# A delta-rule recurrence: the last level of the triangular inverse multiplies its 64x64 blocks alone

## The chip, the core and the metric

The kernel runs on one core of one Trainium2 chip. The metric is the device time in microseconds (us) of one launch, the median over runs. TensorE (PE in the profile; PEld is its weight load) multiplies from SBUF into PSUM; VectorE (DVE) and ScalarE (ACT) read PSUM and compute; GpSimd (POOL) computes on SBUF; SyncE (SP) starts transfers.

## What is computed

The launch computes a whole transformer block with three mixers (attention, a state-space mixer, a gated delta-rule mixer) and then a second block. The change lies in the delta-rule mixer. Cut to what matters:

```
def gdn_mixer(qkv, z, b, a, conv_w, dt_bias, a_log, norm_w):
    ...
    kbeta = kc * betac[..., None]
    strict = jnp.tril(jnp.einsum('bhcid,bhcjd->bhcij', kbeta, kc) * decay, -1)
    rhs = jnp.concatenate([vc * betac[..., None], kbeta * jnp.exp(gc)[..., None]], axis=-1)
    sol = lax.linalg.triangular_solve(strict, rhs, left_side=True, lower=True, unit_diagonal=True)
    u, w = jnp.split(sol, [GDN_HEAD_V], axis=-1)
    ...
    def step(state, inp):
        v_new = u_i - jnp.einsum('bhld,bhde->bhle', w_i, state)
        o = ...
        state = ...
```

There are 1024 tokens and 4 heads. The kernel works with 8 chunks of 128 tokens, so each chunk and head has one 128x128 unit lower triangular matrix whose inverse is wanted.

## The kernel before

All engines walk one list of items, written in `schedule`, each engine issuing in that order its own part of each item. An item of the delta pass is named by a kind and a chunk c:

- `gx` (ACT, L1910): expands the four inverted 32x32 diagonal blocks of chunk c into the 128x128 tiles X (the inverse so far) and XT (its transpose), zero elsewhere.
- `ly` (c, level): TensorE multiplies the triangular matrix (in `SQ[c]`) by X for 4 heads into one PSUM bank (L1467); DVE writes it, times a 0/1 mask of the blocks of that level, to Y (L2499). Level 5 joins 32x32 blocks into 64x64 ones, level 6 joins the two 64x64 blocks into the whole.
- `lx` (c, level): TensorE multiplies Y and X in both orders (L1479), and DVE subtracts the results from X (L2506) and XT (L2508). At level 6 only XT is wanted, so only that product is made.
- `uw` (c): TensorE multiplies the finished XT by the right-hand sides (L1503, then L1506, whose weights have 64 columns and whose result lies on 64 partitions, the halves taken in turn); ACT copies the result (L1921).
- `r1` and `r2` (c): the recurrence. TensorE multiplies by the state (L1513, L1515), DVE makes v_new (`vn`, L2513) and L2514; TensorE multiplies by vn (L1519, L1521); DVE adds up the output (L2518), masks the state's update (L2519) and adds it to the state `Sbd` (L2521). ACT then takes the output's squares (L1897).

The text calls the level 6 items ly6 and lx6, the level 5 items ly5 and lx5. All products are float32, and the trace shows two MATMUL records (passes), each with its weight load, for each such matmul call; an item of 4 heads has 8 passes. The order around the change is fixed by these lines, one round for each chunk c:

```
    for c in range(NT):
        s += at("gx", c + 3) + at("ly", c + 1, 6) + at("r1", c) + at("ly", c + 2, 5) + at("lx", c + 1, 6) + at("r2", c)
        s += at("lx", c + 2, 5) + at("uw", c + 1)
        s += [("gn", n) for n in range(len(NORMED) - 1) if NORMED[n] == c] + [("sn", 1)] * (c == 1)
```

Round c thus begins with ly6 of chunk c+1. `sn` and `gn` are 12 small DVE instructions each, a reciprocal square root of the norms, between two rounds; after `sn`, ACT scales a part of the state-space result (L1893). Ahead of the rounds stands a prologue with ly5, lx5, ly6, lx6 of chunk 0 and uw of chunk 0. Products go round robin through 4 PSUM banks. Before an item an engine waits for the counter of the product or copy that it needs.

Of the kernel before, what the change touches and what calls it, by code (L numbers as in the profile page):

```python
# [19 lines left out]
ALU = mybir.AluOpType  # L20
# [3 lines left out]
P = 128  # L24
# [42 lines left out]
C_ID, C_UP, C_BLK, C_B32, C_LV, C_NEG, C_ALI = 0, 128, 256, 384, 512, 768, 896  # L67
# [254 lines left out]
def build_program(nc, a, out):  # L322
# [166 lines left out]
    with ctx:  # L489
# [14 lines left out]
        con = sbuf("con", [C_END], 96)  # L504
# [58 lines left out]
        SQ = [sbuf(f"SQ{c}", [4, 2, P], 4 * c) for c in range(NT)]  # L563
# [21 lines left out]
        X = [sbuf(f"X{i}", [4, P], 172 + 6 * i) for i in range(3)]  # L585
        XT = [sbuf(f"XT{i}", [4, P], 174 + 6 * i) for i in range(3)]
        Y = [sbuf(f"Y{i}", [4, P], 176 + 6 * i) for i in range(3)]
# [335 lines left out]
        def hslice(c):  # L923
            return slice(c * P, (c + 1) * P)
# [9 lines left out]
        def four(b):  # L934

            return b[:].rearrange("p (h n) -> p h n", h=4)
# [6 lines left out]
        def over(ap, m):  # L943

            return ap.unsqueeze(1).to_broadcast([P, m, ap.shape[1]])
# [250 lines left out]
        def _(pe):  # L1196
            mm, tr = nc.tensor.matmul, nc.tensor.transpose
# [123 lines left out]
            for it in sched:  # L1321
# [11 lines left out]
                elif kind == "cols":  # L1333
                    pe.wait_ge(con_loaded, 16 * 11)
                    b = bank((it, 0))
                    done(tr(b[:, 0:109], rows[0:109, :], ident[0:109, 0:109]), (it, 0))
                elif kind == "norm":
                    stage, hf = j
                    pe.wait_ge(N["diag_ready"], 2 * stage + hf + 1)
                    for k in range(KD):  # L1340
                        b = bank((it, k))
                        for i in range(4):
                            c = 4 * hf + i
                            last = mm(b[:, hslice(i)], norm_row(stage, c)[:, hslice(k)], diag[:, c, :], start=True, stop=True)
                        done(last, (it, k))
                elif kind == "nk":
# [3 lines left out]
                    b = gemm_bank(it)  # L1350
                    for c in range(4):
                        last = mm(b[:, hslice(c)], norm_row(2, c)[:, hslice(j)], diag[:, c, :], start=True, stop=True)
                    last.then_inc(gemm_done[gemm_use[it][1]], 1)
                elif kind == "mx":
# [3 lines left out]
                    for k in range(KD):  # L1358
                        b = bank((it, k))
                        for i in range(4):  # L1360
                            c = 4 * j + i
                            src = atts[:, c, hslice(k)] if k < 2 else xs[:, c, hslice(k - 2)] if k < 6 else qkv[:, c, hslice(k - 6)]
                            last = tr(b[:, hslice(i)], src, ident)
                        done(last, (it, k))
                elif kind == "smT":
                    gemm_consumed(pe, unit_of["sm", 0])
                    b = bank((it, 0))
                    src = stage_of(("sm", 0))[1]
                    for c in range(NT):
                        last = tr(b[:, 16 * c:16 * c + 16], src[0:16, hslice(c)], ident[0:16, 0:16])  # L1370
                    done(last, (it, 0))
                elif kind == "acs":
                    pe.wait_ge(N["da_ready"], 1)
                    pe.wait_ge(rest_loaded, 16)
                    b = bank((it, 0))
# [11 lines left out]
                elif kind == "as":  # L1387
# [3 lines left out]
                    for p in range(2):  # L1391
                        b = bank((it, p))
                        for kv in range(2):
                            last = mm(b[:, kv * 256:kv * 256 + 256], aqT[:, p, hslice(j)], akT[:, kv, j * P:j * P + 2 * P],
                                      start=True, stop=True)
                        done(last, (it, p))
                elif kind == "ap":
                    pe.wait_ge(N["att_exp"], j + 1)
                    for p in range(2):
                        b = bank((it, p))  # L1400
                        for i in range(4):
                            last = tr(b[:, hslice(i)], asb[:, 2 * p + i // 2, hslice(i % 2)], ident)
                        done(last, (it, p))
                elif kind == "ao":
# [5 lines left out]
                    b = bank((it, 0))  # L1410
                    for i in range(4):
                        p, kv = i // 2, i % 2
                        h = p + 2 * kv
                        for s in range(2):
                            last = mm(b[:, h * 64:h * 64 + 64], apT[:, i, s, :], av[:, j + s, kv * 64:kv * 64 + 64],
                                      start=s == 0, stop=s == 1)
                    done(last, (it, 0))
                elif kind in ("pa", "sa"):
                    c = j
                    for key in products_of(it):  # L1420
                        b = bank((it, key))
# [5 lines left out]
                        for h in range(4):  # L1427
                            last = mm(b[:, hslice(h)], da[:, c, 4 * i + h:4 * i + h + 1].to_broadcast([P, P]), upper,
                                      start=False, stop=h == 3)
                        done(last, (it, key))  # L1430
                elif kind == "sg":
                    b = bank((it, 0))
                    for g in range(2):
                        last = mm(b[:, hslice(g)], BC[:, g, hslice(j)], BC[:, 2 + g, hslice(j)], start=True, stop=True)
                    done(last, (it, 0))
                elif kind in ("rk", "rj"):
                    c, z = j, j % 2
                    for key in products_of(it):
                        b = bank((it, key))
                        if key == "kT":  # L1440
# [3 lines left out]
                            for p in range(2):  # L1444
                                last = tr(b[:, hslice(2 + p)], kb[z][:, hslice(p)], ident)
                        elif key == "qT":
                            for p in range(2):
                                last = tr(b[:, hslice(p)], qkv[:, c, hslice(p)], ident)
                        elif key[:2] == "kq":
# [4 lines left out]
                            for h in range(2):  # L1454
                                mm(b[:, h * 256:h * 256 + P], kTp[z][:, 2 * p + h, :], kk[z][:, p, :], start=True, stop=True)
                                last = mm(b[:, h * 256 + P:h * 256 + 256], kTp[z][:, 2 * p + h, :], qT[:, c, p, :], start=True, stop=True)
                        done(last, (it, key))
                elif kind == "ly":
                    c, lv = j
                    z = c % 2  # L1460
# [3 lines left out]
                        side_consumed(pe, (("lx", (c, 5)), "x"))  # L1464
                    b = bank((it, 0))
                    for h in range(4):
                        last = mm(b[:, hslice(h)], SQ[c][:, h, 0, :], X[c % 3][:, h, :], start=True, stop=True)  # L1467
                    done(last, (it, 0))
                elif kind == "lx":
                    c, lv = j  # L1470
# [4 lines left out]
                    for key in products_of(it):  # L1475
                        b = bank((it, key))
                        for h in range(4):
                            l, r = (XT, Y) if key == "x" else (Y, XT)
                            last = mm(b[:, hslice(h)], l[c % 3][:, h, :], r[c % 3][:, h, :], start=True, stop=True)  # L1479
                        done(last, (it, key))  # L1480
                elif kind in ("uw", "yo", "yd", "st", "r1", "r2"):
                    c, z = j, j % 2
# [550 lines left out]
        def _(dve):  # L2033
            step = Steps(dve, dve_step)
            v = nc.vector
# [203 lines left out]
            for it in sched:  # L2239
# [256 lines left out]
                elif kind == "ly":  # L2496
                    c, lv = j
                    b = side_product(dve, (it, 0))
                    step.frees(v.tensor_tensor(Y[c % 3][:], four(b), over(con[:, C_LV + (lv - 5) * P:C_LV + (lv - 4) * P], 4), ALU.mult), (it, 0))  # L2499
                elif kind == "lx":  # L2500
                    c, lv = j
                    z = c % 3
# [2 lines left out]
                        b = side_product(dve, (it, "x"))  # L2505
                        step.frees(v.tensor_tensor(X[z][:], X[z][:], four(b), ALU.subtract), (it, "x"))  # L2506
                    b = side_product(dve, (it, "t"))
                    step.frees(v.tensor_tensor(XT[z][:], XT[z][:], four(b), ALU.subtract), (it, "t"))  # L2508
                elif kind == "r1":
                    c, z = j, j % 2  # L2510
                    side_consumed(dve, (("uw", c), 0))
# [131 lines left out]
```

## Time and profile before

| | |
|---|---|
| time, 3 runs | median 2302.89 us (2302.21 to 2303.53) |
| span of the profiled execution | 2301.8 us |
| TensorE busy | 2126.3 us (92%) |
| VectorE busy | 1236.5 us (54%) |
| the delta pass | from about 516 to 600 us of the span |

The page gives the profiled execution's span and no separate time for it; the span is 1.1 us below the median of the runs. Times in the trace count from the start of the span. The rounds of the delta pass start at 529.5 (c = 0), 540.4, 548.7, 558.1, 569.2, 578.7 and 587.05 us (c = 6); round 7 has only r1 and r2. Behind it stand the transposes for the output projection and the projection itself.

### The profile page before, as it was taken

The numbers are of one execution on the slowest core, as the hardware profiler recorded it, in microseconds if no ns is written. First come the engines' busy times: TensorE is split into PE (matmuls) and PEld (weight loads), VectorE is DVE, ScalarE is ACT, GpSimd is POOL, SyncE is SP. The second block draws the span as 40 slices with busy tenths as digits, with TensorE's granted clock in tenths as the row PEclk, the third lists the DMA queues.
The fourth block names the chain that finished last, engine by engine and source line by source line (L and its number), as shares of the span: only waits on it lengthen the run. The fifth ranks groups of instructions, "written<-read, shape, count | busy, mean of one in ns | idle before, by whom it ended". The sixth has DMA issues, their size and how long they took to land. (4 is left out here: it accounts for less than half of the span.)

```text
span 2301.8 us, 29448 instructions
## 1 busy us (share of the span) xinstructions
PE 2126.3 (92%) x10799; PEld 1783.6 (77%) x10799; DVE 1236.5 (54%) x1827; ACT 864.8 (38%) x1562; POOL 890.8 (39%) x612
## 2 busy tenths in 40 slices
PE   6999998868998999999999968889999999999997
PEld 6788877758886788888877757768888888888886
DVE  4443503866537843444489897679995245110232
ACT  4332216456324434343444544238774122000112
POOL 1232331331345688888832643220000333333334
PEclk9999998889999999999999988999999999999999
DMA  4111310011132122222274534200001111111131
GB/s 147 46 46 46 83 55 19 19 46 38 43 104 85 35 55 65 74 64 74 82 248 142 188 100 147 93 28 1 1 1 33 46 46 37 55 46 47 55 119 73
DMA packets 181824, 157.43 MB, mean 68 GB/s; under 512 B 27589, under 2 KB 147121, under 8 KB 181553
## 3 DMA queue, kind: packets, MB, share of 16 engines
q1 hardware_dynamic: 163904, 119.05, 17.4%
q10 hardware_dynamic: 17776, 36.51, 4.3%
q8 instruction: 86, 1.41, 0.3%
q14 instruction: 58, 0.47, 0.1%
HBM read 134.03 MB, written 21.50 MB: 68 GB/s over the span
## 5 line engine op out<-in xcount | busy, mean ns | idle before, releaser
L1118 POOL TENSOR_SCALAR w_hi<-w_raw 128x1024 fp32r<-128x1024 f32 x91 | 106.0, 1165 | 942.3 <-issue 893.6
L1230 PE MATMUL gemm<-h_hi,w_hi 128*128 128x512 f32 x1072 | 422.4, 394 | 5.6 <-POOL h_lo L1147 5.6
L1232 PE MATMUL gemm<-h_hi,w_lo 128*128 128x512 f32 x1072 | 418.2, 390 | 0.0
L1231 PE MATMUL gemm<-h_lo,w_hi 128*128 128x512 f32 x1072 | 418.0, 390 | 0.0
L1230 PEld LDWEIGHTS gemm<-h_hi,w_hi 128*128 128x128 f32 x1072 | 202.0, 188 | 49.6 <-issue 9.1
L1232 PEld LDWEIGHTS gemm<-h_hi,w_lo 128*128 128x128 f32 x1072 | 201.6, 188 | 42.5
L1231 PEld LDWEIGHTS gemm<-h_lo,w_hi 128*128 128x128 f32 x1072 | 202.1, 189 | 40.4
L1121 POOL TENSOR_TENSOR w_lo<-w_raw,w_hi 128x1024 fp32r<-128x1024 f32 x91 | 230.0, 2527 | 7.6
L870 POOL TENSOR_TENSOR w_lo<-wsum,w_hi 128x512 fp32r<-128x512 f32 x122 | 165.6, 1358 | 83.1 <-ACT w_hi L1682 77.8
L1682 ACT ACTIVATE w_hi<-wsum 128x512 fp32r<-128x512 f32 x155 | 98.1, 633 | 142.0 <-PE gemm L1310 60.8
L1308 PE MATMUL gemm<-h_hi,w_hi 128*128 128x512 f32 x320 | 124.5, 389 | 0.0
L1309 PE MATMUL gemm<-h_lo,w_hi 128*128 128x512 f32 x320 | 124.5, 389 | 0.0
L1310 PE MATMUL gemm<-h_hi,w_lo 128*128 128x512 f32 x320 | 124.5, 389 | 0.0
L2093 DVE SCALAR_TENSOR_TENSOR cacc<-cin,cols,cacc 128x1024 f32<-128x1024 f32 x42 | 67.0, 1596 | 90.1 <-ACT cacc L1630 89.1
L861 POOL TENSOR_TENSOR wsum<-w_raw 128x512 f32<-128x512 f32 x55 | 81.1, 1475 | 79.6 <-DVE w_lo L870 76.3
L870 POOL TENSOR_TENSOR w_lo<-w_raw,w_hi 128x512 fp32r<-128x512 f32 x62 | 88.4, 1425 | 43.8 <-ACT w_hi L1682 26.2
L1308 PE MATMUL gemm<-cmb,w_hi 128*128 128x512 f32 x240 | 94.2, 393 | 2.9 <-POOL w_lo L870 2.9
L1668 ACT ACTIVATE sig<-gemm,cols 128x1024 f32<-128x1024 f32 x16 | 18.0, 1124 | 210.0 <-PE gemm L1232 210.0
L1309 PE MATMUL gemm<-cmb,w_hi 128*128 128x512 f32 x240 | 93.9, 391 | 0.0
L1310 PE MATMUL gemm<-cmb,w_lo 128*128 128x512 f32 x240 | 93.8, 391 | 0.0
L2062 DVE TENSOR_TENSOR PT<-side,PT 128x512 fp32r<-128x512 f32 x128 | 88.5, 691 | 9.9 <-ACT PT L2004 5.9
L2004 ACT ACTIVATE PT<-side 128x512 fp32r<-128x512 f32 x128 | 76.6, 599 | 44.2 <-PE side L1552 39.6
(435 smaller groups left out, 4662.9 us busy)
## 6 DMA issues: line engine op xcount, KB each, us to landing
w_raw<-in_ffn_w_down SPq DMA_DIRECT2D x132, 256.0 KB, 3.1
w_raw<-in_w_in SPq DMA_DIRECT2D x60, 512.0 KB, 3.8
w_raw<-in_ffn_w_gate SPq DMA_DIRECT2D x22, 512.0 KB, 4.0
w_raw<-in_ffn_w_up SPq DMA_DIRECT2D x22, 512.0 KB, 4.1
w_raw<-in_w_out SPq DMA_DIRECT2D x16, 512.0 KB, 3.8
xin<-in_x SPq DMA_DIRECT2D x8, 512.0 KB, 6.9
x<-in_x ACTq DMA_DIRECT2D x1, 4096.0 KB, 15.7
x_spill<-x ACTq DMA_DIRECT2D x2, 2048.0 KB, 6.6
```

The lines of the kernel that those rows point to most:

```text
L861: step(ops.tensor_tensor(wsum[sum_of[n]["buf"]][:], x, y, op), "w_sum" if who == "pool" else "w_sum_v")
L870: ops.tensor_tensor(quarter(wlo, slot), x, quarter(whi, slot), ALU.subtract).then_inc(w_split, 1)
L1118: gp.tensor_scalar(hi[:], raw[key % 4][:], 1.0, 0.0, ALU.mult, ALU.add).then_inc(pool_hi, 1)
L1121: gp.tensor_tensor(lo[:], raw[key % 4][:], hi[:], ALU.subtract).then_inc(w_split, 1)
L1230: mm(o, hi[:, k, m], act[0][:, k, t], start=k == 0, stop=False)
L1231: mm(o, hi[:, k, m], act[1][:, k, t], start=False, stop=False)
L1232: last = mm(o, lo[:, k, m], act[0][:, k, t], start=False, stop=k == kt - 1)
L1308: mm(o, hi[:, k, :], b[0], start=k == 0, stop=False)
L1309: mm(o, hi[:, k, :], b[1], start=False, stop=False)
L1310: last = mm(o, lo[:, k, :], b[0], start=False, stop=k == 3)
L1682: step(af(quarter(whi, slot), x, ACT.Copy), "w_quarter_hi")
L2062: ins = v.tensor_tensor(dst, b, hi, ALU.subtract)
```

## The change

At level 6 only one 64x64 block of each product is not masked off or known: rows 64 to 127, columns 0 to 63 of Y, and in XT rows 0 to 63, columns 64 to 127. The changed kernel multiplies only the 64x64 blocks: ly6 takes its operands from partitions 0 to 63 and writes PSUM partitions 64 to 127; lx6 takes them from 64 to 127 and writes 0 to 63. DVE copies 64 columns for each head on 64 partitions in place of the masked multiplication over 128 (no mask is needed), and writes the negated product to XT's empty block in place of a subtraction over all of XT. Level 5 is as before.

```diff
@@ ly, TensorE
                     for h in range(4):
-                        last = mm(b[:, hslice(h)], SQ[c][:, h, 0, :], X[c % 3][:, h, :], start=True, stop=True)
+                        if lv == 5:
+                            last = mm(b[:, hslice(h)], SQ[c][:, h, 0, :], X[c % 3][:, h, :], start=True, stop=True)
+                        else:
+                            last = mm(b[64:P, h * P:h * P + 64], SQ[c][0:64, h, 0, 64:P], X[c % 3][0:64, h, 0:64], start=True, stop=True)
@@ lx, TensorE
-                            last = mm(b[:, hslice(h)], l[c % 3][:, h, :], r[c % 3][:, h, :], start=True, stop=True)
+                            if lv == 5:
+                                last = mm(b[:, hslice(h)], l[c % 3][:, h, :], r[c % 3][:, h, :], start=True, stop=True)
+                            else:
+                                last = mm(b[0:64, h * P + 64:(h + 1) * P], Y[c % 3][64:P, h, 0:64], XT[c % 3][64:P, h, 64:P], start=True, stop=True)
@@ ly, VectorE
-                    step.frees(v.tensor_tensor(Y[c % 3][:], four(b), over(con[:, C_LV + (lv - 5) * P:C_LV + (lv - 4) * P], 4), ALU.mult), (it, 0))
+                    if lv == 5:
+                        step.frees(v.tensor_tensor(Y[c % 3][:], four(b), over(con[:, C_LV:C_LV + P], 4), ALU.mult), (it, 0))
+                    else:
+                        step.frees(v.tensor_copy(Y[c % 3][64:P, :, 0:64], four(b)[64:P, :, 0:64]), (it, 0))
@@ lx, VectorE
-                    step.frees(v.tensor_tensor(XT[z][:], XT[z][:], four(b), ALU.subtract), (it, "t"))
+                    if lv == 5:
+                        step.frees(v.tensor_tensor(XT[z][:], XT[z][:], four(b), ALU.subtract), (it, "t"))
+                    else:
+                        step.frees(v.tensor_scalar(XT[z][0:64, :, 64:P], four(b)[0:64, :, 64:P], -1.0, None, ALU.mult), (it, "t"))
```

TensorE's order from uw of chunk 0 to r2 of chunk 0, in the kernel before (the last numbers are rows by columns of what is written and the number of matmul calls; tile numbers tell the three buffers of X, XT, Y apart):

```order
L1503 MATMUL side<-kbv_163,XT_155 128x64 x4
L1506 MATMUL side<-XT_155,kbv_163 64x128 x4
L1467 MATMUL side<-X_153,SQ_119 128x128 x4
L1513 MATMUL side<-Sbd,uw_161 128x128 x2
L1515 MATMUL side<-Sbd,qT 128x128 x2
L1467 MATMUL side<-X_154,SQ_120 128x128 x4
L1479 MATMUL side<-XT_156,Y_159 128x128 x4
L1519 MATMUL side<-vn,SQ_118 128x64 x4
```

The same place in the changed kernel, whose line numbers behind the edit are higher:

```order
L1509 MATMUL side<-kbv_163,XT_155 128x64 x4
L1512 MATMUL side<-XT_155,kbv_163 64x128 x4
L1470 MATMUL side<-X_153,SQ_119 64x64 x4
L1519 MATMUL side<-Sbd,uw_161 128x128 x2
L1521 MATMUL side<-Sbd,qT 128x128 x2
L1468 MATMUL side<-X_154,SQ_120 128x128 x4
L1485 MATMUL side<-XT_156,Y_159 64x64 x4
L1525 MATMUL side<-vn,SQ_118 128x64 x4
```

Nothing moved: the third and seventh rows (ly6 and lx6) became 64x64 products, and each now stands between products of other shapes.

VectorE's order from ly6's copy to the state's update, before:

```order
L2499 TENSOR_TENSOR Y_159<-side,con 128x512
L2513 TENSOR_TENSOR vn<-uw_161,side 128x256
L2514 TENSOR_TENSOR o_168<-side,eacs 128x256
L2499 TENSOR_TENSOR Y_160<-side,con 128x512
L2508 TENSOR_TENSOR XT_156<-XT_156,side 128x512
L2518 TENSOR_TENSOR qkv<-o_168,side 128x256
L2519 TENSOR_TENSOR tS<-side,con 128x256
```

and the same in the changed kernel:

```order
L2508 COPY Y_159<-side 64x4x64
L2525 TENSOR_TENSOR vn<-uw_161,side 128x256
L2526 TENSOR_TENSOR o_168<-side,eacs 128x256
L2506 TENSOR_TENSOR Y_160<-side,con 128x512
L2520 TENSOR_SCALAR XT_156<-side 64x4x64
L2530 TENSOR_TENSOR qkv<-o_168,side 128x256
L2531 TENSOR_TENSOR tS<-side,con 128x256
```

Again the order is the same, and the first and the fifth row have 256 elements on each of 64 partitions where they had 512 on each of 128.

## Rows read from the trace of the kernel before

**Rows 1.** The page: the span and the engines' busy time.

```profile
span 2301.8 us, 29448 instructions
...
PE 2126.3 (92%) x10799; PEld 1783.6 (77%) x10799; DVE 1236.5 (54%) x1827; ACT 864.8 (38%) x1562; POOL 890.8 (39%) x612
```

**Rows 2.** Busy time in stretches, by round; PEclk is the granted clock.

```profile
core 0: us, PE busy (x) PEld busy (x) DVE busy (x) ACT busy (x) POOL busy (x), PEclk, DMA share, GB/s
...
540.40:548.70 8.30, 8.30 (x79) 8.06 (x77) 6.34 (x12) 5.21 (x17) 1.84 (x3) 1.00 0.00 0
548.70:558.10 9.40, 8.55 (x78) 8.14 (x76) 8.34 (x24) 6.52 (x14) 1.84 (x3) 1.00 0.01 2
558.10:569.20 11.10, 8.57 (x78) 8.16 (x76) 6.38 (x12) 7.96 (x29) 1.84 (x3) 1.00 0.00 1
...
587.00:594.70 7.70, 6.28 (x58) 5.80 (x55) 5.20 (x14) 2.59 (x10) 0.00 (x0) 1.00 0.00 0
594.70:601.50 6.80, 6.10 (x29) 5.83 (x28) 3.57 (x14) 0.97 (x6) 4.03 (x6) 0.50 0.01 2
```

**Rows 3.** Timeline of TensorE's weight loads, 538 to 549 us.

```profile
538.73 0.97 PEld L1503 LDWEIGHTS side<-kbv,XT 128*128 128x128 f32 x8
539.77 0.42 PEld L1506 LDWEIGHTS side<-XT,kbv 128*64 128x64 f32 x8
540.36 0.97 PEld L1467 LDWEIGHTS side<-X,SQ 128*128 128x128 f32 x8 [0.17 <-DVE X L2506]
541.24 0.53 PEld L1513 LDWEIGHTS side<-Sbd,uw 128*128 128x128 f32 x4
...
542.14 0.97 PEld L1467 LDWEIGHTS side<-X,SQ 128*128 128x128 f32 x8
543.03 0.97 PEld L1479 LDWEIGHTS side<-XT,Y 128*128 128x128 f32 x8
543.92 0.97 PEld L1519 LDWEIGHTS side<-vn,SQ 128*128 128x128 f32 x8
...
548.68 0.97 PEld L1467 LDWEIGHTS side<-X,SQ 128*128 128x128 f32 x8 [0.17 <-DVE X L2506]
```

**Rows 4.** What TensorE waited for, 516 to 602 us.

```profile
PE side L1467 <- ACT XT L1910: 4.6, 2, 2.4
PE side L1513 <- issue: 2.5, 1, 2.5
PE side L1479 <- DVE Y L2499: 1.8, 2, 0.9
```

**Rows 5.** Timeline of VectorE, end of round 1 and into round 2.

```profile
545.64 0.42 DVE L2518 TENSOR_TENSOR qkv<-o,side 128x256 f32<-128x256 f32 x1 [0.62 <-PE side L1521]
...
546.56 1.27 DVE L2521 SCALAR_TENSOR_TENSOR Sbd<-Sbd,cdc,tS 128x128 f32<-128x128 f32 x2
547.86 0.69 DVE L2506 TENSOR_TENSOR X<-X,side 128x512 f32<-128x512 f32 x1
...
549.30 0.17 DVE L2048 TENSOR_SCALAR nv<-nss_s 128x8 f32<-128x8 f32 x1
...
551.53 0.17 DVE L2054 SCALAR_TENSOR_TENSOR nrs_s<-nt__74,nrs_s 128x8 f32<-128x8 f32 x1
551.73 0.69 DVE L2499 TENSOR_TENSOR Y<-side,con 128x512 f32<-128x512 f32 x1
```

**Rows 6.** Timeline of ScalarE in rounds 2 and 3.

```profile
551.79 4.30 ACT L1893 ACTIVATE xs<-xs,nrs_s 128x256 f32<-128x256 f32 x8 [2.33 <-DVE nrs_s L2054]
...
561.11 0.60 ACT L1921 ACTIVATE uw<-side 128x512 f32<-128x512 f32 x1
```

**Rows 7.** VectorE's groups by shape, whole span: mean ns of one.

```profile
L2062 DVE TENSOR_TENSOR qp<-side,qp 64x512 fp32r<-64x512 f32 x16 | 11.1, 695 | 7.4 <-ACT qp L1979 7.1
...
L2457 DVE COPY qT<-side 128x256 f32<-128x256 f32 x8 | 3.4, 425 | 17.7 <-PE side L1448 17.7
```

**Rows 8.** The one line whose products use few rows of the array.

```profile
L1370 PE MATMUL side<-con,cacc x8: 207/208/230, 229.2 to 229.7; 16*128 16x16 f32 x8
```

## Prediction

> **What bounds the kernel.** I read the page first: TensorE is busy for 92% of a span of 2301.8 us [rows 1], so the first question for a change to TensorE's work is whether its own stretch is also TensorE's. The table by rounds says so, with exceptions. Round 1 (540.4 to 548.7) has TensorE busy 8.30 of 8.30 us at the full clock, 2.4 GHz (PEclk 1.00); rounds 2 and 3 take 9.40 and 11.10 us for the same 8.6 us of products [rows 2]. Then the waits: in the whole delta pass TensorE waits 4.6 us for ACT's expansion of X and XT, 2.5 us (once) at L1513, and 1.8 us (twice) for Y [rows 4]. The 2.5 us stand under "issue", but the timeline names the cause: L1513 reads uw, and ACT's copy of it ran at 561.11 to 561.71, behind ACT's 4.30 us of L1893 [rows 6]. So a shorter product pays where TensorE is back to back, and is lost just before one of these waits. The reader should also see a second loop almost as long as TensorE's: behind r2, DVE runs L2518 (545.64), L2519, two of L2521 and L2506 until 548.55, and ly6 of the next round needs that last one; its weights load at 548.68 [rows 5, 3]. This loop starts at r2's end, so what r2 gains it gains too: it caps nothing that comes ahead of r2.
>
> **What the change takes away on TensorE.** An item of 8 passes with full tiles takes 0.88 to 0.89 us from its first weight load to the next item's (540.36 to 541.24, 542.14 to 543.03, 543.03 to 543.92) [rows 3]. 16 such items (ly6 and lx6 of 8 chunks) become 64x64. No row of before shows a 64x64 product. The nearest is L1506: 64 columns of weights, all 128 rows, 8 loads within 0.42 us [rows 3]; I take 0.055 a pass, 0.44 an item. The other neighbour, L1370, has 16 rows and 128 columns of weights: 8 passes start within 0.5 us, some 0.065 each [rows 8], so 0.5 an item. The upper bound is that nothing shrinks (0.89): L1506's passes go to two halves of the array in turn, the new ones all to the same quarter, and if a load could then not run beside the product before it, the time would stay. The lower bound is half my value, 0.22, if the two passes of a call could run side by side. I take 0.44, since L1506's moving operand has 128 columns and the new one 64, which leaves room even where each tile works alone. The saving is 0.45 an item.
>
> **What it adds on TensorE.** Going from full tiles into narrow ones and back is not free. From L1503's first load (538.73) to L1513's (541.24) are 2.51 us; 2 x 0.89 of it is full items and 0.43 is L1506's, so 0.30 is left for two changes of shape, 0.15 each [rows 3]. ly6 stands behind L1506, so before it there was a change already; it adds one, on leaving. lx6 stands between full items and adds two, unless TensorE waits ahead of it anyway and the entry hides in the wait. So in a round that TensorE bounds ly6 gives 0.45 - 0.15 = 0.30 and lx6 0.45 - 0.30 = 0.15.
>
> That is a rule of the skill too, and it speaks against the change. The Trainium skill, "TensorEngine Tiling (Array Packing)", section Key Properties, says that a change of the tiling mode, as against a change of tile within one mode, drains TensorE; it gives no price. The trace agrees, with 0.15 us for each change. Without the drains the change would be worth 0.45 at every item, with them two thirds of that at ly6 and one third at lx6. The Trainium skill, "TensorE: Matmul & The Clock Gate", section LDWEIGHTS, has a load's time go with its columns (P/1.2 ns) and not with its rows: 64 columns would be 53 ns, an estimate of 0.43 us for 8, beside L1506's 0.42.
>
> **VectorE.** The two instructions of level 6 go from 512 elements a partition to 256. A copy of 128x256 out of PSUM takes 425 ns, and one of 64x512 takes 695 ns, as long as the 690 of the full ones [rows 7, 5], so the gain is in the columns and not in the partitions: 0.27 each, 4.3 us over 16. DVE is busy 6.34 of 8.30 us in round 1 [rows 2]; XT's write has lx5 and most of uw's time ahead of its reader, so it gives nothing on the path. Y's copy is on the path only where DVE is late: in rounds 2 and 4, where `sn` and `gn` keep DVE from 549.30 to 551.70 (and 2.5 us at 569.8) and lx6 waits 0.9 us for Y [rows 5, 4]. Scheduling, waits, banks and transfers are as before.
>
> **The sum by rounds** (what comes through to the end of the pass):
> - Prologue: ly6, ly5, lx6, lx5 of chunks 0 and 1. TensorE alone would gain 0.45; lx5's wait for DVE's copy of ly5's product leaves about 0.27. uw of chunk 0 and with it ACT's expansion behind it come 0.27 earlier.
> - Round 0: ly6 stands ahead of a wait for ACT of 2.2 us (half of the 4.6) and is lost, lx6 gives 0.15.
> - Round 1: 0.30 + 0.15 = 0.45. Here DVE's `sn` hangs on it, and so ACT's long chain.
> - Round 2: Y's copy 0.27 and lx6 0.30 (its entry hides in the wait), but all of it, and ly6 of round 3, is lost in the wait for ACT at 561.8, which runs from 551.79 without a gap [rows 6]. 0.
> - Round 3: lx6 0.15.
> - Round 4: 0.27 + 0.30 = 0.57. Round 5: 0.45.
> - Round 6: no ly5 between r1 and lx6, so Y's copy is just late as well (587.05 on): about 0.6.
> Together 0.27 + 0.15 + 0.45 + 0.15 + 0.57 + 0.45 + 0.60 = 2.6 us. By 16 items alone it would be 16 x 0.45 = 7.2, less 24 new changes of shape, 3.6: about half is paid for drains and another 1 us is lost ahead of ACT.
>
> Behind the pass TensorE goes on with transposes and projections without another engine's fixed date, so I let all of it through: 2301.8 - 2.6 = 2299.2 for the span, and 1.1 more, the distance of span and median, for the time: **2300.3 us**. A measurement of this kernel can tell about 0.2% (4.6 us) from no change, so this counts as no change.
>
> **Rivals.**
> - *The narrow passes do not shrink* (0.89 an item). For it: all four heads use the same quarter of the array. Against it: the trace shows loads running beside products everywhere. Then every ly6 costs 0.15 and lx6 0.30 more; prologue 0.45, rounds 0, 1, 3, 4, 5, 6: 0.30, 0.45, 0.30, 0.15, 0.45, 0.45, together 2.5 us slower: 2305.4. It decides from the point where an item takes over 0.7 us; at 1.1 us an item it would be slower by over 0.2%.
> - *The clock falls in a gap that gets longer.* After a stretch with waits TensorE's granted clock fell to 0.50, 1.2 GHz, from 594.7 to 601.5 [rows 2]. Round 3's gap of 2.5 us becomes about 3.4 (0.30 of ly6 and 0.57 of round 2 lie ahead of it), and the clock held there before (PEclk 1.00). A stretch like that one, 6.8 us at half speed, costs 3.4 us where TensorE has work all the time, and one half as long 1.7: 2302.0 to 2303.7, the gain gone. Before, the clock fell behind the waits at the end of the pass and in none of the longer gaps ahead of it (rounds 0 and 3), so a longer gap is a risk and no more. The Trainium skill, "TensorE: Matmul & The Clock Gate", section HAM oscillation, has TensorE fall back to half its clock when it sits idle between bursts, and start the next burst slow; by it the longer gap of round 3 would cost what this rival says. The rows show the fall at 594.7 and none at round 3's gap.
> - *The two passes of a call run side by side* (0.22 an item). 0.22 more at the 11 items that come through: 2297.9.
> - *The gain never leaves the pass*, because a transfer or POOL's weight split sets the next stage: 2302.9. Nothing in the delta pass's neighbourhood shows TensorE waiting for POOL.
>
> **How the numbers follow.** My forecast 0.58; the clock 0.17; passes that do not shrink 0.10; side by side 0.07; gain lost behind 0.05; the rest 0.03. Range 2297.4 to 2304.8: it takes in all but the whole of the first rival and what lies beyond; my forecast's own range is 2299.2 to 2301.4 (0.5 an item or 0.4, a switch at 0.12 to 0.18). Only the side-by-side case comes near to faster by over 0.2% (2298.3): 0.07. Slower by over 0.2% needs passes over 1.1 us an item or two clock falls: 0.04. The same: 0.89.
>
> **What would show it.** In the trace of after: ly6's 8 loads to the next item's first load 0.59 us, lx6's 0.59 with 0.15 ahead of it; Y's and XT's level 6 instructions 0.42 us; rounds 1 and 5 at 7.9 us where they took 8.3; `sn` starting 0.87 earlier (548.4); the gap at L1519 (once L1513) in round 3 grown to 3.4; PEclk 1.00 from 520 to 594. I am wrong if items of 64x64 take 0.89, if changes of shape cost over 0.22 each (then lx6 gives nothing), or if the clock row changes.

## The result and the profile after

The changed kernel takes 2307.63 us (median of 12 runs), the kernel before 2302.29 us in the same comparison: ratio 1.0024, 95% interval 1.0016 to 1.0032. It is slower, by 5.3 us between the medians (0.24% by the ratio), where I forecast 2.6 us less, and outside my range. Two of the 12 runs of before took 3542.58 and 7460.52 us and are left out of the ratio.

The page of after shows TensorE busy 4 us longer than in [rows 1], although the change takes work from it:

```profile
span 2306.2 us, 29448 instructions
...
PE 2130.2 (92%) x10799; PEld 1784.7 (77%) x10799; DVE 1232.6 (53%) x1827; ACT 865.5 (38%) x1562; POOL 890.1 (39%) x612
```

Where that comes from stands in the table of stretches, cut at the rounds (as [rows 2]; rounds 0 to 5):

```profile
core 0: us, PE busy (x) PEld busy (x) DVE busy (x) ACT busy (x) POOL busy (x), PEclk, DMA share, GB/s
...
527.30:542.60 15.30, 12.81 (x79) 11.91 (x76) 6.02 (x12) 8.43 (x25) 1.84 (x3) 0.67 0.15 53
542.60:550.80 8.20, 8.00 (x78) 7.45 (x76) 5.24 (x11) 5.21 (x17) 1.84 (x3) 1.00 0.00 0
550.80:559.70 8.90, 8.07 (x79) 7.46 (x77) 7.86 (x24) 6.03 (x13) 1.84 (x3) 1.00 0.01 2
559.70:573.40 13.70, 10.12 (x78) 9.45 (x76) 5.80 (x12) 8.47 (x30) 1.84 (x3) 0.75 0.00 1
573.40:582.40 9.00, 8.07 (x78) 7.45 (x77) 7.96 (x24) 5.32 (x17) 2.68 (x5) 1.00 0.00 1
582.40:590.60 8.20, 8.00 (x79) 7.46 (x77) 5.86 (x12) 2.00 (x9) 6.37 (x10) 1.00 0.01 3
```

Round 0 of before, for comparison:

```profile
529.50:540.40 10.90, 8.65 (x79) 8.20 (x77) 5.99 (x12) 8.42 (x25) 1.84 (x3) 1.00 0.20 74
```

Read the PEclk column first. Rounds 0 and 3 were granted 0.67 and 0.75 of the full clock, that is, 1.2 GHz for part of them; in before every round from 529.5 to 594.7 had 1.00 ([rows 2] and the line above). From ly6's first load to the next round's, round 0 takes 15.3 us where it took 10.8, and round 3 takes 13.7 where it took 11.1: 7.1 us together. The other rounds up to the fifth are shorter than before: rounds 1 and 5 8.2 for 8.3, round 2 8.9 for 9.4, round 4 9.0 for 9.5. So the change does save TensorE's time, and loses more in two rounds in which the clock falls. From the first load of uw of chunk 0 to the first load of the output projection the pass takes 83.6 us where it took 78.3: 5.3 us, the whole of the difference between the medians. (Ahead of that the profile of after is 2.2 us shorter, behind it 1.2 us longer.)

This is not one unlucky profile. Every run lists its mean granted clock: 0.967 to 0.970 in the 12 runs of after, 0.973 to 0.975 in the 33 runs of before that stand beside the first experiments.

TensorE's weight loads in round 1 of after, the place of [rows 3]:

```profile
542.03 0.42 PEld L1512 LDWEIGHTS side<-XT,kbv 128*64 128x64 f32 x8
542.62 0.54 PEld L1470 LDWEIGHTS side<-X,SQ 64*64 64x64 f32 x8 [0.17 <-issue]
543.47 0.52 PEld L1519 LDWEIGHTS side<-Sbd,uw 128*128 128x128 f32 x4 [0.31 <-issue]
543.91 0.53 PEld L1521 LDWEIGHTS side<-Sbd,qT 128*128 128x128 f32 x4
544.35 0.97 PEld L1468 LDWEIGHTS side<-X,SQ 128*128 128x128 f32 x8
545.45 0.54 PEld L1485 LDWEIGHTS side<-XT,Y 64*64 64x64 f32 x8
546.05 0.97 PEld L1525 LDWEIGHTS side<-vn,SQ 128*128 128x128 f32 x8
```

lx6 (L1485) takes 0.60 us to the next item (545.45 to 546.05), and its entry makes the item ahead of it 1.10 long in place of 0.89: 0.81 for 0.89, a saving of 0.08. ly6 (L1470) has the same eight passes and yet takes 0.85 (542.62 to 543.47), against 0.88 before. The row behind it says "0.31 <-issue". ScalarE's timeline at the same place names the wait:

```profile
542.80 0.60 ACT L1927 ACTIVATE uw<-side 128x512 f32<-128x512 f32 x1 [3.07 <-PE side L1512]
```

The copy of uw ends at 543.40, and r1 (L1519) reads that copy: it loads at 543.47. Before, ly6's 0.88 us happened to fill just that time (539.77 to 541.24 from uw's second half to r1, 1.47 us, [rows 3]; 542.03 to 543.47, 1.44 us, now). r1 cannot start earlier, whatever ly6 takes; TensorE waits 0.20 us instead.

What TensorE waited for in the delta pass, as [rows 4]:

```profile
PE side L1468 <- ACT XT L1916: 4.6, 2, 2.4
PE side L1519 <- issue: 4.6, 6, 3.6
PE side L1519 <- ACT uw L1927: 1.7, 2, 1.4
PE side L1485 <- DVE Y L2508: 1.4, 2, 0.7
```

The waits of r1 (L1519) went from 2.5 and 1.4 us to 4.6 and 1.7; round 3's alone is 3.6.

### The profile page after: what moved, and what is told of

Same layout as the page of the kernel before. It is cut to its first block and busy times, and to the rows that moved or that the text cites. A ratio compares the mean times of both kernels' runs of the same rounds, so it can differ in the third digit from the quotient of the medians.

```text
span 2306.2 us, 29448 instructions
## 1 busy us (share of the span) xinstructions
PE 2130.2 (92%) x10799; PEld 1784.7 (77%) x10799; DVE 1232.6 (53%) x1827; ACT 865.5 (38%) x1562; POOL 890.1 (39%) x612
## 6 DMA issues: line engine op xcount, KB each, us to landing
x<-in_x ACTq DMA_DIRECT2D x1, 4096.0 KB, 15.9
```

## The experiments

The theory after the first look: the narrow products save little (r1 waits for ScalarE anyway, lx6 pays for two changes of shape), and TensorE, less busy around the two long waits for ScalarE, has its clock lowered there (A). Rivals: the longer waits alone do it (B); the loss lies behind the pass (C). Each kernel below was run 11 times and timed against before on the same chip: e1 to e4, e5 to e8, e9 to e12, and e13 with e14 are four such groups, and between groups only the ratios compare. The clock is each run's mean granted clock, the median over the runs; before has 0.974 or 0.975. The ratios' intervals are some 0.09% (2 us) to each side.

| run | time, us | before, us | ratio (95%) | clock |
|---|---|---|---|---|
| the change | 2307.63 | 2302.29 | 1.0024 (1.0016 to 1.0032) | 0.968 |
| e1 VectorE's part only | 2301.12 | 2301.92 | 0.9994 (0.9985 to 1.0003) | 0.975 |
| e2 lx6 narrow, ly6 full | 2302.30 | 2301.92 | 1.0002 (0.9994 to 1.0011) | 0.975 |
| e3 ly6 narrow, lx6 full | 2303.99 | 2301.92 | 1.0011 (1.0003 to 1.0020) | 0.971 |
| e4 64 columns, 128 rows | 2306.84 | 2301.92 | 1.0024 (1.0015 to 1.0033) | 0.969 |
| e5 before, two gaps filled | 2301.57 | 2301.72 | 0.9999 (0.9990 to 1.0008) | 0.974 |
| e6 the change, two gaps filled | 2300.67 | 2301.72 | 0.9995 (0.9986 to 1.0004) | 0.972 |
| e7 before, ly5 ahead of r1 | 2306.16 | 2301.72 | 1.0015 (1.0006 to 1.0023) | 0.972 |
| e8 the change, ly5 ahead of r1 | 2302.82 | 2301.72 | 1.0005 (0.9996 to 1.0014) | 0.974 |
| e9 before, level 6 of two heads | 2302.74 | 2301.68 | 1.0005 (0.9996 to 1.0014) | 0.972 |
| e10 the change, round 0 filled | 2303.05 | 2301.68 | 1.0008 (0.9999 to 1.0017) | 0.973 |
| e11 the change, three gaps filled | 2298.90 | 2301.68 | 0.9989 (0.9980 to 0.9998) | 0.975 |
| e12 as e11, ly5 ahead of r1 | 2301.31 | 2301.68 | 0.9998 (0.9989 to 1.0007) | 0.975 |
| e13 before, three gaps filled | 2301.01 | 2300.76 | 0.9999 (0.9990 to 1.0008) | 0.973 |
| e14 as e11, ly6 full | 2300.05 | 2300.76 | 0.9995 (0.9986 to 1.0004) | 0.973 |

### e1 to e4: one part of the change alone

e1 leaves TensorE's products full; only VectorE's two instructions are narrow.

```diff
-                            last = mm(b[64:P, h * P:h * P + 64], SQ[c][0:64, h, 0, 64:P], X[c % 3][0:64, h, 0:64], start=True, stop=True)
+                            last = mm(b[:, hslice(h)], SQ[c][:, h, 0, :], X[c % 3][:, h, :], start=True, stop=True)
...
-                                last = mm(b[0:64, h * P + 64:(h + 1) * P], Y[c % 3][64:P, h, 0:64], XT[c % 3][64:P, h, 64:P], start=True, stop=True)
+                                last = mm(b[:, hslice(h)], Y[c % 3][:, h, :], XT[c % 3][:, h, :], start=True, stop=True)
```

> TensorE's level 6 products are full 128x128 again, only VectorE's two level 6 instructions are the narrow ones. Theory A (the narrow products themselves bring TensorE's granted clock down in rounds 0 and 3, which costs some 7 us): no fall of the clock between 520 and 590 us, time as before or 0.3 to 1 us below it (Y's copy is 0.27 us shorter in rounds 2, 4 and 6). Theory B (the clock falls because the waits ahead of ScalarE got longer, whatever the products): round 3's gap grows by 0.27 us at most, so a fall in round 3 in some profiles, time 0 to 3 us above before. Theory C (the loss lies behind the delta pass and has nothing to do with it): 2 to 3 us above before.

Measured: the time of before, clock 0.975. Its profile, which is of the fastest of the 11 runs, has PEclk 1.00 in rounds 0, 1 and 3. The loss is TensorE's part. C falls: the rest of the kernel is as in after, and the change's 5.3 us lie in the pass itself (83.6 us for 78.3).

e2 has the first of the two edits above, e3 the second.

> ly6 is full on TensorE, lx6 is 64x64, VectorE as in the change. ly6 stands directly ahead of the gaps of rounds 0 and 3, lx6 behind them. Theory A: with ly6 full ahead of the gap the clock holds at the gap's start as before, so most of the loss goes: 0 to 2 us above before, rather below. If both kinds count alike, half of the loss, some 2.5 us. Theory B: the gaps shrink back by 0.3 us, to 2.2 and 3.2 us, a fall in round 3 only: 1 to 3 us above before. Round 1 takes 8.2 us as in the change, since the copy of uw on ScalarE, not ly6, sets r1's start.

> ly6 is 64x64, lx6 is full. Theory A: the stretch before each gap holds the narrow item, so the clock falls in rounds 0 and 3 nearly as in the change, 3 to 5 us above before. Theory B: the same gaps as in the change, the same falls, 4 to 5 us above before. Round 1 takes 8.3 us as before: ly6's saving of 0.3 us is spent waiting for ScalarE's copy of uw, and lx6 costs 0.89.

e2 is as fast as before, with its clock. In its profile the clock fell in round 3 (PEclk 0.67; the round takes 15.8 us) and not in round 0; but it did not fall at the end of the pass either (PEclk 1.00 from 585 to 612), where before's profile spends 6.8 us at half clock. So two profiles with nearly the same mean clock (0.975 and 0.973) can have their falls in different places. e3 is slower by 2.1 us, clock 0.971, less than either theory had it (3 to 5); its profile, of the slowest of its runs, has falls in round 0 (0.75) and round 3 (0.76). So narrow ly6, the item ahead of both gaps, brings a part of the loss, and narrow lx6 alone none that can be told. Both together lose 5.3 us; whether that is more than the sum of the parts is inside the intervals. The times of the items came as expected: round 1 takes 8.23 us with lx6 narrow, 8.27 with ly6 narrow, 8.18 with both, 8.32 before.

e4 keeps 64 columns and contracts over all 128 partitions:

```diff
-                            last = mm(b[64:P, h * P:h * P + 64], SQ[c][0:64, h, 0, 64:P], X[c % 3][0:64, h, 0:64], start=True, stop=True)
+                            last = mm(b[64:P, h * P:h * P + 64], SQ[c][:, h, 0, 64:P], X[c % 3][:, h, 0:64], start=True, stop=True)
...
-                                last = mm(b[0:64, h * P + 64:(h + 1) * P], Y[c % 3][64:P, h, 0:64], XT[c % 3][64:P, h, 64:P], start=True, stop=True)
+                                last = mm(b[0:64, h * P + 64:(h + 1) * P], Y[c % 3][:, h, 0:64], XT[c % 3][:, h, 64:P], start=True, stop=True)
```

> Both level 6 products have 64 columns of weights but all 128 rows, as L1512 has. Gaps and item lengths as in the change, twice as much of the array in use. Theory A: if what counts is how much of the array works, the falls are fewer or shorter than in the change, 1 to 4 us above before; if any narrow product counts alike, 5 us above. Theory B: as the change, 5 us above before. For change of shape: ly6 now follows L1512 in the same shape and its entry costs nothing, but r1 waits for ScalarE's copy of uw anyway, so round 1 stays at 8.1 to 8.2 us.

It is the change over again: 1.0024, clock 0.969, and round by round, from uw to uw, the same times within 0.02 us. The 64 partitions of the operands are worth nothing; all that the change saves comes from the 64 columns. That twice as much of the array works does not help the clock either.

### e5, e6 and e10: products into the gaps

If the clock is the loss, idle-time work that nobody reads must give it back. The products go to a PSUM bank of the next stage, in program order ahead of that stage's own first write:

```diff
                 elif kind == "ly":
                     c, lv = j
                     z = c % 2
+                    if j == (2, 5):
+                        banks_free(pe, ("wo", 0, 0))
+                        fb = gemm_bank(("wo", 0, 0))
+                        for w in (512, 512, 256):
+                            mm(fb[:, 0:w], ident, con[:, 0:w], start=True, stop=True)
...
                     elif kind == "r1":
+                        if c == 3:
+                            banks_free(pe, ("wo", 0, 0))
+                            fb = gemm_bank(("wo", 0, 0))
+                            for w in (512, 512, 512):
+                                mm(fb[:, 0:w], ident, con[:, 0:w], start=True, stop=True)
                         side_consumed(pe, (("uw", c), 0))
```

> The kernel before, with products that nobody reads in two places where TensorE waits for ScalarE: ahead of ly5 of chunk 2 (round 0; float32, 512, 512 and 256 columns, about 2.2 us at the full clock) and ahead of r1 of chunk 3 (round 3; three of 512 columns, 2.6 us). They are added work in idle time. Theory A (the clock gives what the change lost): the clock does not fall between 520 and 590 in before either, so the time is that of before, 0 to 1 us below it, and the mean granted clock 0.974 or a little more. Theory B (the filler only delays what follows): 0.5 to 2 us above before.

> The changed kernel with the same idle-time products in the same two places. Theory A: no fall of the clock in rounds 0 and 3 (15.3 and 13.7 us in the change's profile become some 10.8 and 11.2), the mean granted clock goes from 0.968 to 0.974 or more, and the time lands 1 to 2 us below before, which is what the narrow products save. Theory B (the narrow products and their changes of shape are slower by themselves): the clock may rise, the time stays 2 us or more above before.

> The changed kernel with the idle-time products in round 0's gap only. It splits the loss between the two gaps. In the change's profile round 0 took 15.28 us where it takes 10.74 without a fall and round 3 13.73 for 11.5: so filling round 0 alone should take back some 4.5 of the 7 us, leaving the time 1 to 2 us above before, with the clock at 0.971. If round 3 alone made the loss: still 4 us above before.

In before the fillers change nothing (0.9999). In the change they take back 6.7 us by the ratios (1.0024 to 0.9995): it is now 1 us below before, not told from it. Its stretches, rounds 0, 1 and 3:

```profile
527.70:538.40 10.70, 10.36 (x84) 8.50 (x82) 5.35 (x12) 8.42 (x25) 1.84 (x3) 1.00 0.21 76
538.40:546.60 8.20, 8.00 (x80) 7.45 (x76) 5.85 (x12) 5.21 (x17) 1.84 (x3) 1.00 0.01 2
555.50:567.00 11.50, 10.75 (x84) 8.50 (x82) 5.81 (x12) 8.48 (x30) 1.84 (x3) 1.00 0.01 1
```

More work on TensorE (84 matmul records for 78 or 79 in rounds 0 and 3), the clock at 1.00, and 4.6 and 2.2 us less time than the change's 15.3 and 13.7. From uw of chunk 0 to uw of chunk 7 e6 takes 62.1 us, before 63.4 and the change 68.9: the 6.8 us between e6 and the change are the 6.7 us of the ratios. Its mean clock rose to 0.972 only, where I expected 0.974 or more; with the clock at 1.00 in both rounds that remainder is not explained. With round 0 alone filled (e10) 3.7 us come back by the ratios (1.0024 to 1.0008), and its profile still has round 3 at 15.9 us with PEclk 0.68. So both gaps count; which of them counts for more is inside the intervals. e6 settles the cause of the loss: the narrow products are not slower, the clock is.

### e7 and e8: ly5 ahead of r1

```diff
-        s += at("gx", c + 3) + at("ly", c + 1, 6) + at("r1", c) + at("ly", c + 2, 5) + at("lx", c + 1, 6) + at("r2", c)
+        s += at("gx", c + 3) + at("ly", c + 1, 6) + at("ly", c + 2, 5) + at("r1", c) + at("lx", c + 1, 6) + at("r2", c)
```

> The kernel before with ly5 of chunk c+2 ahead of r1 of chunk c in every round, so that a whole item stands between uw and r1. Theory (r1's start is set by ScalarE's copy of uw, 1.44 us behind the start of uw's second half): before, ly6's 0.89 us just about filled that wait, so nothing is gained: within 1 us of before, or 0.5 to 2 us slower, since vn now has only lx6 to hide behind. Rival (r1 waits for the change of shape): the same time, but round 1 stays 8.3 us in the changed kernel in this order too.

> The changed kernel in that same order. Theory (ScalarE's copy of uw swallows what ly6 saves): with ly5 between ly6 and r1, ly6 takes 0.60 us up to the next item in place of 0.85, and round 1 takes some 7.9 us where the change has 8.18 and before 8.32. Rival (the change of shape back to full tiles costs 0.31 us behind ly6): ly6 stays at 0.85 and round 1 at 8.2. The clock still falls in rounds 0 and 3 (gaps as long or longer), so the time stays 3 to 6 us above before.

Weight loads of e8 in round 1:

```profile
539.42 0.54 PEld L1470 LDWEIGHTS side<-X,SQ 64*64 64x64 f32 x8 [0.17 <-DVE X L2515]
540.02 0.97 PEld L1468 LDWEIGHTS side<-X,SQ 128*128 128x128 f32 x8
540.91 0.53 PEld L1519 LDWEIGHTS side<-Sbd,uw 128*128 128x128 f32 x4
541.36 0.53 PEld L1521 LDWEIGHTS side<-Sbd,qT 128*128 128x128 f32 x4
542.00 0.54 PEld L1485 LDWEIGHTS side<-XT,Y 64*64 64x64 f32 x8
542.75 0.97 PEld L1525 LDWEIGHTS side<-vn,SQ 128*128 128x128 f32 x8 [0.20 <-issue]
```

ly6 now takes 0.60 us (539.42 to 540.02) in place of 0.85, and r1 starts without a wait: the 0.25 us were the wait for uw's copy, not the change of shape. But the round takes 8.08 and not the 7.9 that I expected: r2 (L1525) now loads 0.20 us late, and in round 2 its products wait 0.60 us for VectorE's vn, which r2 reads and which is made from r1's product, with less work of TensorE between the two. In before the order (e7) costs 4.4 us by the medians and 3.4 by the ratio, more than I expected: ly5 no longer fills time behind r1, so round 0's wait for XT grows from 2.25 to 3.13 us, and the clock falls there; rounds 2 and 4 are longer too. e8 is not told from before, 1.1 us above it, and 4 us better than the change in its own order, clock 0.974; I had expected no such gain. The new order moves the waits: in e8's profile round 0's is 3.62 us, with a fall that is shorter than the change's (the round takes 13.2 us for 14.9, uw to uw), and round 3's is down from 3.58 to 0.21 us, with no fall; a fall came in round 2 instead. The likely source of the gain is the long wait that is gone, and it does not tell A from B.

### e9: full tiles, less work

Level 6 of two heads of four is computed on TensorE, on full 128x128 tiles; the other two heads' products are left out.

```diff
-                    for h in range(4):
+                    for h in range(4 if lv == 5 else 2):
                         last = mm(b[:, hslice(h)], SQ[c][:, h, 0, :], X[c % 3][:, h, :], start=True, stop=True)
...
-                        for h in range(4):
+                        for h in range(4 if lv == 5 else 2):
```

> The kernel before, but TensorE computes the level 6 products of two of the four heads only; the other two are left out (VectorE still reads and writes all four). The items take some 0.45 us in place of 0.89, all on full 128x128 tiles, with no change of shape. It tells what brings the clock down. Theory A1 (TensorE's busy time ahead of and behind the gap is what counts): falls in rounds 0 and 3 as in the change, mean granted clock 0.969 to 0.971, time 2 to 5 us above before. Theory A2 (products on a part of the array count less, or the change of shape does it): mean clock 0.974 as before, no more falls in rounds 0 and 3 than before has, time 1 to 2.5 us below before, since each lx6 saves 0.45 us.

Rounds 0, 1 and 3 of its profile:

```profile
527.40:539.20 11.80, 9.35 (x70) 8.80 (x68) 5.88 (x12) 8.41 (x25) 1.84 (x3) 0.86 0.22 81
539.20:547.00 7.80, 7.64 (x72) 7.26 (x68) 6.34 (x12) 5.21 (x17) 1.84 (x3) 1.00 0.00 0
556.10:569.70 13.60, 10.25 (x71) 9.82 (x69) 6.41 (x12) 8.32 (x30) 1.84 (x3) 0.75 0.00 0
```

There is no narrow product in it and no change of shape at level 6, and the clock falls in the same two rounds (0.86 and 0.75; mean 0.972 over the runs). Round 1 is the shortest of all, 7.83 us, and still the time is not below before's: leaving out half of the level 6 products made nothing faster. The result lies between my two expectations (clock 0.969 to 0.971, or 0.974), and on the side of the first: no narrow product is needed for a fall. e9 also has TensorE less busy than the change and yet the higher clock (0.972 for 0.968) and the shorter round 0 (11.8 for 15.3), so narrow products may count for less than their busy time. That part was not isolated.

What the two falls hang on shows when the waits of all profiles in the old order without a filler in round 3 are put side by side (us; r1 of chunk 0 and ly5 of chunk 2 in round 0, r1 of chunk 3 in round 3):

| profile | ahead of r1, round 0 | ahead of ly5, round 0 | PEclk, round 0 | ahead of r1, round 3 | PEclk, round 3 |
|---|---|---|---|---|---|
| before | none | 2.25 | 1.00 | 2.53 | 1.00 |
| e1 VectorE's part only | none | 2.24 | 1.00 | 2.79 | 1.00 |
| e2 lx6 narrow | none | 2.25 | 1.00 | 3.08 | 0.67 |
| e3 ly6 narrow | 0.24 | 2.25 | 0.75 | 3.27 | 0.76 |
| e9 two heads | 0.21 | 2.25 | 0.86 | 3.35 | 0.75 |
| e10 round 0 filled | 0.24 | filled | 1.00 | 3.57 | 0.68 |
| the change | 0.24 | 2.25 | 0.67 | 3.58 | 0.75 |
| e4 64 columns | 0.38 | 2.25 | 0.67 | 3.64 | 0.75 |

Round 0 of the change in TensorE's timeline, and of before behind it:

```profile
528.26 0.68 PE L1519 MATMUL side<-Sbd,uw 128*128 128x128 f32 x4 [0.24 <-ACT uw L1927]
531.64 2.08 PE L1468 MATMUL side<-X,SQ 128*128 128x128 f32 x8 [2.25 <-ACT XT L1916]
...
533.82 1.16 PE L1467 MATMUL side<-X,SQ 128*128 128x128 f32 x8 [2.25 <-ACT XT L1910]
```

In round 0 the long wait is the same everywhere, and the clock fell in just those profiles in which ly6 ahead of it is shorter and leaves a second, small wait ahead of r1: that is A, and the item that counts is ly6 (e2 and e3). What stands behind the wait does not: in the change's profile the clock is at half speed from 531.4 on, ahead of ly5's restart at 531.64. In round 3 the order is that of the long wait itself: the clock held at 2.53 and 2.79 us and fell at 3.08 and more, with ly6 full (e2) or short. There B is enough, and A is not shown. Each row is one profile, and no run moved a gap in time without changing what stands beside it, so that the moment of the gap plays a part is not excluded.

### e11 to e14: a third filler

A third filler stands ahead of r1 of chunk 7, where before's profile (0.50 from 594.7 to 601.5, [rows 2]), after's and several of the experiments' had a further fall:

```diff
+                        if c == 7:
+                            banks_free(pe, ("wo", 0, 0))
+                            fb = gemm_bank(("wo", 0, 0))
+                            for w in (512, 256):
+                                mm(fb[:, 0:w], ident, con[:, 0:w], start=True, stop=True)
                         side_consumed(pe, (("uw", c), 0))
```

> The changed kernel with idle-time products in three gaps: rounds 0 and 3 as in the run before, and 768 columns (1.3 us) ahead of r1 of chunk 7, where the clock falls in all profiles but one (594 to 601 us). Theory: that fall costs some 2 us in r2 and the transposes behind it, so if it goes the time is 2 to 4 us below before, mean clock 0.975 or more. If the fall there has its cause in the waits behind r1 (for vn, 1.3 us), it stays and the time is that of the kernel with two gaps filled, 1 us below before.

> The same three fillers and ly5 of chunk c+2 ahead of r1 of chunk c. Round 1 took 8.08 us in that order and 8.18 in the old one, but rounds 2 and 4 wait longer for Y: within 1 us of the run with three fillers in the old order, and the clock as there.

> The kernel before with the three fillers. If the narrow products are worth what the rounds of the two-filler profiles say (63.4 us against 62.1 us from the first uw to the last, and 0.3 in the prologue), this stays 1.5 us above the changed kernel with three fillers, at 2300 to 2301. If the third filler alone makes the gain: 2298 to 2299.5, as fast as the changed kernel with it.

> lx6 narrow, ly6 full on TensorE, VectorE's narrow instructions, three fillers. If ly6's narrow form saves nothing, since r1 waits for uw's copy anyway: as the changed kernel with three fillers, 2298.5 to 2300. If it does save something: 1 us above that.

e11 is faster than before, if narrowly: 2298.90 against 2301.68 us, 0.9989 (0.9980 to 0.9998). Before with the same three fillers (e13) is 0.9999, as it was with two (e5), so the fillers show no gain in before. What the narrow products are worth once the clock holds is then 2.3 us by these two ratios, and 0.9 us by the pair with two fillers (e6 and e5); neither is clear of the intervals. The profiles say 1.3 us from the first uw to the last (62.1 for 63.4 us, the same in both pairs).

That the third filler adds anything is not shown: e11's interval overlaps that of e6 (0.9986 to 1.0004). In e11's own profile the clock still falls, later, behind a wait of 1.87 us for VectorE (PEclk 0.73 from 597 to 600, 0.71 from 600 to 603), while e12, e13 and e14 hold it with the same wait. e1, e2 and e10 had no fall at the end of the pass without any filler there. What decides at this place stays open.

With ly6 full (e14) the ratio is 0.9995; whether the narrow ly6 adds to e11 is inside the intervals. The order with ly5 first (e12) gives nothing: 0.9998, 2.4 us above e11 where I expected 1 at most. Its round 3 has no long wait for the filler to stand in (0.21 us in e8), and takes 11.5 us with it for 8.9 without, uw to uw.

## Why the prediction was wrong

- **What bounds the pass**: right in the main. TensorE is back to back in rounds 1 and 5 of before, and ly6 of rounds 0 and 3 is lost ahead of ScalarE.
- **The narrow item**, 0.44 plus its exit, 0.59 in all: measured 0.60. Right, and so was the reading that the columns count: e4 shows that the rows add nothing.
- **ly6's 0.30 in a round that TensorE bounds**: wrong, 0.03. The missing term is ScalarE's copy of uw. It stood in rows that I had read ([rows 3] and the timeline of ScalarE): r1 needs it, and it ends 1.4 us behind the start of uw's second half, just where ly6 ended (in round 2 of before 549.46, with r1's load at 549.57). I took r1 as following ly6 because its weights loaded without a gap; it was a tie. e8 takes the tie apart. The wait of 0.20 to 0.24 us that is left in ly6's place also stands ahead of the fall in round 0.
- **lx6's 0.15**: 0.08, since the entry costs 0.21 and not 0.15. The Trainium skill, "TensorEngine Tiling (Array Packing)", section Key Properties, has a change of tiling mode drain TensorE. This trace agrees that a change costs time: 0.21 us in and some 0.14 out, an estimate (0.60 less eight passes of 0.058, from the 0.54 us of lx6's loads).
- **VectorE's terms**: right in size (428 and 416 ns for 690); rounds 2 and 4 gained 0.54 and 0.55, near the 0.57 forecast for each; round 2's is spent in round 3's wait, as forecast.
- **The sum without the clock**: too large. I added 2.4 us for rounds 0 to 6 (2.6 with the prologue). With the clock at 1.00 in all of them (e6) 1.3 us come through, mainly because rounds 1 and 5 give 0.14 us each and not 0.45, and round 6 0.23 and not 0.60 (the prologue gave 0.15 to 0.31 for 0.27 in the profiles). That e11 lies 2.8 us below before, near my 2.6, is chance and no confirmation.
- **The step that failed**: the sum had the granted clock stay at 1.00 from 520 to 594. It was among the rivals, with a chance of 0.17, in round 3 only and at 1.7 to 3.4 us. It fell in rounds 0 and 3: 15.3 and 13.7 us where the filled kernel e6 has 10.7 and 11.5, so the clock cost 4.6 and 2.2 us. Round 3 went as that rival had it, in place and in size: the wait grew to 3.58 us (forecast 3.4), and the clock held at 2.53 and 2.79 us and fell at 3.08 and more in the profiles. I gave it too small a chance, since the clock had held at the shorter gap. Round 0 I had not seen. I had looked only for a gap that gets longer, and this one did not (2.25 us of wait for XT, as before); what changed is that TensorE has less work just ahead of it. e9 shows that less work there, on full tiles, is enough for a fall in round 0.
- The Trainium skill, "TensorE: Matmul & The Clock Gate", section HAM oscillation, has TensorE go back to half its clock when it idles between bursts. The trace agrees as to the kind of place (0.67 and 0.75 in the two rounds with the long waits). The length of the wait is not all that counts in these traces: a wait of 2.25 us held the clock in before and not in the change, and at the end of before's pass it fell behind 1.42 us of wait, after a stretch as full as 6.28 of 7.70 us (587.0 to 594.7, [rows 2]).

What stays open: why the fall in round 0 lasts 10 us in the change (PEclk 0.67) and shorter in e3 and e9, that is, how much a narrow product counts for the clock; and why the clock falls at the end of the pass in some profiles (before, the change, e3 to e9) and not in others (e1, e2, e10). The latter is why e2 could fall in round 3 and still have before's mean clock.

## What to carry to other kernels

Where TensorE's granted clock is full but its stretch has waits like the 2.25 and 2.53 us here, work taken from TensorE ahead of these waits can cost more than it saves, by lengthening the wait or by thinning the work before it: compare the mean granted clock of all runs before the items' times, and try cheap products in the gap as a test. One profile shows where the clock fell in one execution; only the runs show whether that is the rule. Before a product is shortened, look at what the next item waits for, on every engine, and at ties above all: an item that starts without a gap may be held by two things at once. A 64-column product next to full tiles pays about 0.2 us on the way in, so 8 passes save 0.08 us and not 0.45.

## What the runs showed of the hardware

- Added work made the kernel faster: two fillers in the change's gaps took the ratio to before from 1.0024 to 0.9995, three to 0.9989, and neither did anything in before (0.9999).
- In round 3 the granted clock held at waits of 2.53 and 2.79 us and fell at 3.08 to 3.64 (six profiles); in round 0 a wait of 2.25 us held it with full ly6 ahead and not with a shorter one.
- Half of the level 6 products left out (e9) gained nothing (1.0005), and the clock fell in two rounds.
- With 64 columns of weights, 128 rows take what 64 rows take (from the first uw to the last: 68.9 us both).
- The mean granted clock of a run tells kernels apart whose times differ by 0.24%: 0.968 or 0.969 in the two slowest, 0.974 or 0.975 in before. It does not rank the rest: e6 has 0.972 and is no slower than before.
